# Hybrid decoder step on one core: attention probabilities normalised on VectorE in place of GpSimd, sample states two slots earlier, scores in fp32

## Time and profile before

| | us |
|---|---|
| median of 3 runs | 1066.13 (1063.52 to 1066.85) |
| the profiled execution | 1063.2 |
| its span, first to last instruction | 1061.4 |
| PE busy | 1010.1 (95%) |
| DVE busy | 631.4 (59%) |
| ACT busy | 386.8 (36%) |
| POOL busy | 428.8 (40%) |
| mean granted clock of TensorE | 0.991 |

### The profile page before, as it was taken

The page is one execution under the profiler, slowest core; times in us unless marked ns, Lnnn a source line. Parts: engine busy times, 40 slices in busy tenths (PEclk is TensorE's granted clock), DMA queues, the critical chain, the costliest instruction groups (busy, mean ns, idle before and its releaser), DMA issues.

```text
span 1061.4 us, 22401 instructions
## 1 busy us (share of the span) xinstructions
PE 1010.1 (95%) x9360; PEld 944.2 (89%) x9360; DVE 631.4 (59%) x1195; ACT 386.8 (36%) x775; POOL 428.8 (40%) x286
## 2 busy tenths in 40 slices
PE   6999999999999999999999999999989999898996
PEld 4899999999999998899999999999988888777895
DVE  8153746555564737456743234367667878977835
ACT  4412313132313133545332233510047757654522
POOL 1244545545545454612135342344535334322243
PEclk9999999999999999999999999999989989999998
DMA  7111213030312222012233324211112113322103
GB/s 284 41 61 41 86 39 104 21 104 24 102 63 64 71 73 83 22 43 63 103 105 136 120 80 145 77 46 58 40 57 63 59 56 101 91 71 61 50 34 127
DMA packets 50533, 81.39 MB, mean 77 GB/s; under 512 B 15425, under 2 KB 34433, under 8 KB 50305
## 3 DMA queue, kind: packets, MB, share of 16 engines
q1 hardware_dynamic: 50432, 79.97, 23.1%
HBM read 62.35 MB, written 17.60 MB: 75 GB/s over the span
## 4 chain that ended last, share of the span: by engine, by line
PE 71%; DVE 15%; ACT 7%; issue 5%; POOL 1%; DMA 0%; DVEq 0%; SPq 0%; ACTq 0%; POOLq 0%
PE G L1592 51%; PE G L1842 5%; DVE SP L1429 4%; ACT SP L1009 4%; PE R L1645 3%; DVE VK L1172 3%; DVE QNL L1414 3%; PE R L1691 2%; PE R L1619 1%; PE R L1684 1%; PE R L1670 1%; DVE PT L1447 1%; PE R L1667 1%; PE G L1696 1%; PE R L1631 1%
## 5 line engine op out<-in xcount | busy, mean ns | idle before, releaser
L1592 PE MATMUL G<-XH,WH 128*128 128x344 f32 x1176 | 385.8, 328 | 1.9 <-DVE RAWF L1105 1.9
L1592 PE MATMUL G<-XL,WH 128*128 128x344 f32 x1176 | 378.0, 321 | 2.4 <-DVE KE L1399 1.9
L1592 PE MATMUL G<-XH,WL 128*128 128x344 f32 x744 | 237.7, 319 | 0.0
L1592 PEld LDWEIGHTS G<-XH,WH 128*128 128x128 f32 x1176 | 221.9, 189 | 6.0 <-issue 2.4
L1592 PEld LDWEIGHTS G<-XL,WH 128*128 128x128 f32 x1176 | 221.7, 189 | 5.0 <-DVE WL L1095 2.2
L643 POOL TENSOR_TENSOR WL<-WR,WH 128x1024 fp32r<-128x1024 f32 x40 | 104.3, 2608 | 178.8 <-ACT WH L782 178.8
L782 ACT ACTIVATE WH<-WR 128x1024 fp32r<-128x1024 f32 x58 | 61.1, 1055 | 261.1 <-PE G L1592 166.7
L1592 PEld LDWEIGHTS G<-XH,WL 128*128 128x128 f32 x744 | 139.8, 188 | 0.0
L1592 PE MATMUL G<-XL,WL 128*128 128x344 f32 x432 | 139.2, 322 | 0.0
L674 POOL TENSOR_TENSOR K<-K,FP 128x512 f32<-128x512 f32 x48 | 78.1, 1627 | 104.6 <-PE R L1645 104.6
L720 POOL TENSOR_TENSOR SP<-SP,small 128x1024 f32<-128x1024 f32 (+1 forms) x32 | 57.3, 1792 | 135.1 <-DVE small L1440 135.1
(11 more groups left out here) (251 smaller groups left out, 1940.6 us busy)
## 6 DMA issues: line engine op xcount, KB each, us to landing
WR<-w SPq DMA_DIRECT2D x58, 512.0 KB, 3.5
A<-x SPq DMA_DIRECT2D x8, 516.0 KB, 8.6
RESO<-x SPq DMA_DIRECT2D x8, 516.0 KB, 4.6
h_spill<-H SPq DMA_DIRECT2D x8, 516.0 KB, 2.9
gate_spill<-EV SPq DMA_DIRECT2D x24, 172.0 KB, 1.9
RES<-h_spill SPq DMA_DIRECT2D x24, 172.0 KB, 2.6
y<-H SPq DMA_DIRECT2D x24, 172.0 KB, 1.9
SS<-states SPq DMA_DIRECT2D x8, 512.0 KB, 5.0
```

The lines of the kernel that those rows point to most:

```text
L1592: return nc.tensor.matmul(G[unit_bank(NU * n + i)][:, 0:TU], w[:, n % 3, k, :], x[:, seg(i)], start=(k == 0 and p == 0), stop=(k == KT - 1 ...
```

## The change

1. The probabilities are normalised on DVE, by four `tensor_scalar` instructions (one per head, 256 or 128 columns) at the end of `denominators`, behind a wait for the reciprocal; POOL's `normalise` goes.
2. `decode_state` and `decode_add` are run in slot 6 instead of slot 8, ahead of `chunk_states`; the sample values are stored transposed (`[b, e]`), and VK reads `VD` contiguously.
3. The scores are one fp32 product from `A` and a negated copy of the keys `KNEG`; QNH, QNL, KBH, KBL, both `cut_queries` and their semaphores go.
4. `cut_slice`'s subtraction (the low part of late gated outputs) is done by POOL.

```diff
-    vs_d = nc.dram_tensor("sample_values", [HEADS, P, DEC], fp32, kind="Internal").ap()
+    vs_d = nc.dram_tensor("sample_values", [HEADS, DEC, P], fp32, kind="Internal").ap()
...
-    KBH, KBL = sb("KBH", [P, SEQ], fp32r, rb_), sb("KBL", [P, SEQ], fp32r, rb_)
+    KNEG = sb("KNEG", [P, SEQ], fp32, rb_)
...
-            sp.dma_start(vs_d[r], RAWV[:, SEQ:T]).then_inc(vs_out, 16)
+            sp.dma_start(vs_d[r].rearrange("b e -> e b"), RAWV[:, SEQ:T], allow_slow_non_contiguous=True).then_inc(vs_out, 16)
...
-            sp.dma_start(VD[:, 0:SEQ], vs_d[r].rearrange("e b -> (e b)").unsqueeze(0).broadcast_to([P, SEQ])
+            sp.dma_start(VD[:, 0:SEQ], vs_d[r].rearrange("b e -> (b e)").unsqueeze(0).broadcast_to([P, SEQ])
...
-        def normalise(q):
-            keys = slice(P if q % NC == 0 else 0, 2 * P)
-            pool.wait_ge(rd_done, q + 1)
-            sp_ = SP_[q % 2][:, :, keys]
-            nc.gpsimd.tensor_tensor(sp_, sp_, small[:, q % 2, 4, :].unsqueeze(2).broadcast_to(
-                [P, 4, keys.stop - keys.start]), ALU.mult).then_inc(p_done, 1)
...
+        def cut_slice(q):
+
+            pool.wait_ge(slice_hi, q - 15)
+            nc.gpsimd.tensor_tensor(pair(AR, q), pair(A, q), pair(XL, q).bitcast(fp32), ALU.subtract
+                                    ).then_inc(slice_lo, 1)
+
+        for s in range(-3, NQ + 1):
+            if s >= 17:
+                cut_slice(s - 1)
...
-        nc.scalar.activation(KBH[:], KE[:, 0:SEQ], ACT.Copy).then_inc(kb_high, 1)
+        nc.scalar.activation(KNEG[:], KE[:, 0:SEQ], ACT.Copy, scale=-1.0).then_inc(kb_done, 1)
...
-            if s + 3 < NQ:
-                cut_queries(s + 3)
...
-                                        VD[:, 0:SEQ].rearrange("p (e b) -> p b e", b=DEC)[:, 4 * i:4 * i + 4],
+                                        VD[:, half(i)].rearrange("p (b e) -> p b e", b=4),
...
                     if slot == 8:
+                        chunk_states(r)
+                    if slot == 6:
                         decode_state(r)
                         decode_add(r)
-                        chunk_states(r)
...
-        dve.wait_ge(kb_high, 1)
-        nc.vector.tensor_tensor(KBL[:], KE[:, 0:SEQ], KBH[:].bitcast(fp32), ALU.subtract).then_inc(kb_done, 1)
...
             nc.vector.reciprocal(sm[:, 4, :], sm[:, 2, :]).then_inc(rd_done, 1)
+            dve.wait_ge(rd_done, q + 1)
+            keys = slice(P if q % NC == 0 else 0, 2 * P)
+            for i in range(4):
+                ins = nc.vector.tensor_scalar(SP_[q % 2][:, i, keys], SP_[q % 2][:, i, keys], sm[:, 4, i:i + 1], None, ALU.mult)
+            ins.then_inc(p_done, 1)
...
-            pe.wait_ge(qn_done, q + 1)
             if q:
                 pe.wait_ge(sc_read, 2 * q)
+            else:
+                pe.wait_ge(q_rot, HP)
+                pe.wait_ge(kb_done, 1)
             for jj in range(2):
-                for n, (a, k) in enumerate(((QNH, KBH), (QNH, KBL), (QNL, KBH))):
-                    for v in range(2):
-                        rows = slice(64 * v, 64 * v + 64)
-                        ins = nc.tensor.matmul(R[v][:, 2 * P * jj + keys.start:2 * P * (jj + 1)], a[rows, q % 2, jj, :],
-                                               k[rows, tok], start=(n == 0), stop=(n == 2))
+                for v in range(2):
+                    rows = slice(64 * v, 64 * v + 64)
+                    ins = nc.tensor.matmul(R[v][:, 2 * P * jj + keys.start:2 * P * (jj + 1)], pair(A, q)[rows, jj],
+                                           KNEG[rows, tok], start=True, stop=True)
                 ins.then_inc(sc_done, 1)
```

More of the change, by code:

```diff
@@ L200, in build @@
     rb_ = [rest]
-    KBH, KBL = sb("KBH", [P, SEQ], fp32r, rb_), sb("KBL", [P, SEQ], fp32r, rb_)
-    rfree = [rb_[0]]
+    KNEG = sb("KNEG", [P, SEQ], fp32, rb_)
+    rb_[0] += 4 * SEQ
     rb_[0] += 2 * 4 * SEQ
@@ L212, in build @@
     PT = sb("PT", [P, 2, 512], fp32, rb_)
-    QNH, QNL = sb("QNH", [P, 2, 2, P], fp32r, rb_), sb("QNL", [P, 2, 2, P], fp32r, rb_)
+    rb_[0] += 2 * 4 * 4 * P
     SGR = sb("SGR", [P, 2, 2, P], fp32, rb_)
@@ L309, in build @@
     k_out = sem("k_out")
-    kb_high = sem("kb_high")
     kb_done = sem("kb_done")
@@ L342, in build @@
     sg_in = [sem(f"sg_in{i}") for i in range(2)]
-    qn_high = sem("qn_high")
-    qn_done = sem("qn_done")
     sc_done = sem("sc_done")
@@ L737, in _ @@
         prepare(N_B2 + 2)
-        for s in range(-3, NQ):
-            if 0 <= s + 1 < NQ:
-                normalise(s + 1)
+        def cut_slice(q):
[5 more added lines that the diff above has]
+                cut_slice(s - 1)
             for n in range(N_B2 + 3, N_BO):
@@ L994, in _ @@
             prepare(N_BQ + j + 2)
[L996 to L1002, removed]
         def exponentials(q):
@@ L1409, in _ @@
         dve.wait_ge(q_rot, HP)
[L1411 to L1415, removed]
         def minima(q):
@@ L1454, in gate_output @@
                                     ALU.mult).then_inc(gated, 1)
[L1456 to L1459, removed]
         def first_half(t):
@@ L1491, in _ @@
                 copy_own(s)
[L1492 to L1495, removed]
             if 0 <= s + 2 < NQ:
@@ L1867, in _ @@
             if s == 0:
-                pe.wait_ge(kb_done, 1)
                 pe.wait_ge(vp_done, 2)
```

## The result

| | before | after |
|---|---|---|
| median of 13 runs each, us | 1064.16 (1062.46 to 1066.85) | 1072.53 (1068.72 to 1077.09) |
| ratio | | 1.0078, 95% interval 1.0062 to 1.0094 |
| span of the profiled execution, us | 1061.4 | 1071.1 |
| DMA packets under 512 B | 15425 | 22592 |
| mean granted clock | 0.991 | 0.986 |

What follows compares the result with a forecast made beforehand. PE's unit products (51% of the chain) bound the kernel, with a DVE/ACT ring in attention. Terms +1.7, -0.8, -8.4 and +2.3 gave -5.2 us: 1058.0 or 1060.9, middle 1059.5, range 1049 to 1070.

Steps and rivals of the forecast that it cites:

- Hidden, up to a landing of about 20 us: Recurrence, SP: the transposed store delays nothing, since slot 6 comes some 25 us after.
- rival D: Recurrence: sample values land over 20 us late, slot 6 waits, heads lose their gain; 1068 or more, chance 0.03.
- ST stall, -8.4: Recurrence, end of each head: PE no longer waits for the chunk states ST; -8.4 us over eight heads.
- Last iteration, +2.3: Slot 6, last iteration: norm queued behind moved work ends late, PE waits for ACT's square; +2.3 us, bounds 0 and 3.3.
- fp32 scores, 1.05: Attention, PE: four two-pass fp32 matmuls replace twelve fp32r ones and take 1.05 us a step; upper bound 1.9.
- rival B: Attention, PE: fp32 passes on the two row halves do not overlap, steps of 7.0 to 7.1; 1072 us, chance 0.12.
- rival C: Attention, DVE: tensor_scalar runs one element a cycle, 0.28 us more in 28 steps; 1067.5 us, chance 0.13.
- Normalise on DVE: Attention ring: four tensor_scalar cost 1.20 us for QNL's 1.33; -0.14 a wide step, +1.7 in all with contact.
- Contact: Attention steps 1, 2, 3, 6, 12, 13: POOL's gate product delays tensor_scalar by 0.95; each step loses 0.81, +4.9 us.
- The weight gain of step 2: Attention step 2: it follows POOL's gate product and may block DVE once more; 0 to 1.7, counted +0.9 us.
- Rival A: Attention: no contact, POOL's gate product never meets the normalise on DVE; 1053 us, chance 0.22.
- The sum: Whole kernel: +1.7 for the normalise, -0.8 first scores, -8.4 ST, +2.3 last iteration; -5.2 us.

Runs made afterwards that it cites:

- e15: Kernel before plus, per head, an extra load of 1024 pieces of 4 B from DRAM into a spare SBUF tile; 1065.24 us.
- e6: Kernel before plus, per head, an extra transposed store of the sample values, 1024 pieces of 4 B side by side in DRAM; 1078.29 us.
- e14: e6 with one sample of eight in the extra store, 128 pieces of 4 B a head; 1078.11 us.
- e5: e1 with the norm of head 4 ahead of the decode in slot 6 of the last iteration; 1053.64 us.
- e3: Kernel before with items 1, 3 and 4 alone (normalise on DVE, fp32 scores, late low parts on POOL); 1062.65 us.
- e2: Kernel before with only the transposed store and contiguous VK, decode still in slot 8; 1067.15 us.
- e1: Changed kernel with sample values stored as [e, b] again and VK strided; 1058.55 us.
- e8: e5 with POOL's gate products from step -1 on held until that step's normalisation is done; 1049.74 us.
- e16: Changed kernel with sample values stored as [e, b] but VK still contiguous, so values in the wrong order; 1057.44 us.
- e13: e6 with the extra store's 1024 pieces of 4 B placed 64 B apart in DRAM; 1064.85 us.
- e11: Control for e6: kernel before plus the same extra store as [e, b], 128 pieces of 32 B a head; 1064.41 us.
- e12: e6 with four of the eight samples in the extra store, 512 pieces of 4 B a head; 1081.75 us.

## Why the prediction was wrong, step by step

- **The step that failed** is "On SP the transposed store of the sample values becomes 1024 elements of 4 B; the mirror transfer [...] lands in 2.3 us", with its conclusion "Hidden, up to a landing of about 20 us". After with and without it is 1.0078 against 0.9931 of the kernel before: +15.6 us, where I had 0. From the issue of the store to that of the VD load it is 10.4 to 11.6 us in the eight heads. Two errors lie in it. The nearest row scattered into SBUF, and the store scatters into DRAM; e15 shows that the first direction is free, and e6 and e14 that the second isn't. And I asked only who waits for the data (slot 6, in fact in time: rival D did not happen). What else goes over the DMA engines meanwhile I didn't ask, and it was POOL, DVE and PE that stopped.
- **ST stall, -8.4.** Right in place and size: seven gaps of 1.22 us are gone, and e5, which is e3 with the decode in slot 6 and no stall in the last iteration, is 8.5 us below e3 by the two changes (-11.2 and -2.7). e2 adds that contiguous VK suffice for it.
- **Last iteration, +2.3.** Right: 2.22 us. The upper bound (3.3 "with a slow VK") is e1's: 3.07 idle, 3.34 from start to start. Not in the sum: the clock behind the stop. e5 against e1 gives 4.9 us for the removal of both.
- **fp32 scores, 1.05.** Right: the eight records take 1.13 us above, so the halves of the rows overlap; rival B did not happen. tensor_scalar 348 ns for 0.35; rival C did not happen.
- **Normalise on DVE.** The late step was 6.34 for 6.35. Contact: 1, 3, 5, 6, 9 and 13, six steps, as many as I had counted, but 5 and 9 in place of 2 and 12; that the number agrees is luck. One more is at step -1 (a piece of 1.02 us). A step cost 0.53 over the 6.49 of before, not 0.81: POOL's product lay where I had it (0.91 to 1.84 behind the denominators), but the third piece ended at 1.97, soon after it, and not a whole piece later, so that contact adds 0.68 and not 0.95. The weight gain of step 2 cost nothing (+0.9 in the sum). These two make 2.6 of the 3.6 us by which e3's -2.7 is better than my +0.9 for attention. Rival A (no contact) was false in the changed kernel; e8 makes it true by hand and gains 3.9 over e5's six contacts (-1, 1, 5, 6, 9 and 13).
- **The sum** of -5.2 has e16's -7.4 (-5.8 to -9.1) beside it, without the store: 2.2 us too small and just outside the interval. With what the runs gave for the terms, -8.4 for ST, +2.2 in the last iteration and some 1.6 of clock behind it (4.9 less e1's stop of 3.3), and -2.7 for attention, it is -7.3. The rest of the working stood, in part because two errors of opposite sign stand in it (attention 3.6 too dear, the clock left out); one term of 0 was 15.6.

The Trainium skill ("DMA: Bandwidth & Descriptors", Back-pressure in remote DMA) says of transfers between cores that a stalled write also stalls the other queues of its DMA engine. This is a store to DRAM on one core, so the page doesn't speak of it. What the traces here have looks like it: the VD load of e14 lands in 7.0 us (e13: 4.1), and the packet of the instruction queue in after takes 3.3 (before: 1.1).

**What stays open.** That the store costs the time is shown by its removal (e1, e16) and its addition (e6, e14). That POOL, DVE and ACT stop because their instructions come late over the DMA engines is only argued, from the releaser that the trace can't name, the slow packets of the instruction queue, and the common restart with SP. The slow packets don't cover every stop: at 171.0 and 275.2 in after POOL stops, and the packets there took 1.5 and 1.2 us. Nor is every stop the store's: e16 has one of PE of 1.29 us, on "issue". No run stopped the instructions in another way. Why half the samples cost as much as all or more, and why a head is spared in one execution and hit in the next, is not settled. Nor is the distance between 4 B and 64 B at which neighbours stop hurting, nor the size of a piece: 128 side by side cost 13.1 us with 4 B each (e14) and nothing with 32 B (e11).

## What to carry to other kernels

Size a transfer by a row with the same side scattered, and ask of a bad one not only who waits for its data but what else moves over the DMA engines while it hangs. When two edits of one ring come together, price each alone: here one (-10.0) paid for the other (+8.8), and the best kernel (-20.6 us) keeps the fp32 scores, slot 6 and the late low parts, with POOL normalising, the old store and the norm ahead of the decode. An instruction that is moved in one engine's order needs its place checked in the last iteration too: the norm ahead of the decode was worth 4.9 us.

## What the runs showed of the hardware that I had not expected

- 4-byte pieces from different partitions that fall side by side in DRAM cost 13 to 16 us over eight heads, whether they are 128, 512 or 1024 a head. In the changed kernel the queue that waits for them goes on 6.1 to 7.7 us after the last recorded piece (0.5 to 1.0 in the kernel before). 64 B apart, or towards SBUF, 1024 of them cost nothing measurable.
- Engines that wait for none of this data stop in that time: POOL up to 8.83 us and DVE up to 2.12 in the changed kernel, 9.10 and 6.19 in e12 (some 3 us of POOL's are ordinary). Packets of the instruction queue took up to 3.3 us in the changed kernel and 6.2 in e14, where the kernel before has none above 1.6.
- Three of PE's six stops behind the store in the changed kernel (up to 3.2 us) are followed by products at the lower clock (0.66 and 0.68 over two stretches of 5 us), which adds 1.5 us where it was measured. It isn't every stop: e12 has one of 3.1 us, at 233, with full clock behind it.
